# Three products on constant tables ahead of TensorE's wait for the second up matrix of every expert

## The reference

```
def expert_block(args):
    xb, e = args
    hb = jax.nn.silu(xb @ w1[e]) * (xb @ w3[e])
    return hb @ w2[e]
```

## Time and profile before

| | before |
| --- | --- |
| median of three runs | 1366.91 us |
| the profiled execution, its own time | 1372.07 us |
| its span, first to last instruction | 1370.3 us |
| mean granted TensorE clock | 0.956 |
| TensorE busy | 1131.5 us, 83% |
| DMA queue of SyncE | 458.01 MB, 81.6% of 16 engines' span |
| matrix products with up matrices (line 884) | 154.2 + 126.8 us in the two largest groups |

### The profile page before, as it was taken

The page is one execution under the profiler, slowest core; times in us unless marked ns, Lnnn a source line. Parts: engine busy times, 40 slices in busy tenths (PEclk is TensorE's granted clock), DMA queues, the critical chain, the costliest instruction groups (busy, mean ns, idle before and its releaser), DMA issues.

```text
span 1370.3 us, 34053 instructions
## 1 busy us (share of the span) xinstructions
PE 1131.5 (83%) x14903; PEld 712.7 (52%) x14903; DVE 402.2 (29%) x1111; ACT 231.4 (17%) x616; POOL 12.8 (1%) x28
## 2 busy tenths in 40 slices
PE   8999789867767778869999999988987677677794
PEld 4444355544444445548887557445554444454552
DVE  1254522211111111134468735043221111111123
ACT  0133211100000001123533114111110000001011
POOL 0000000000000000020000000000000000000000
PEclk9999999999999999979999999999999999999997
DMA  9924599999999999993335324589999999999995
GB/s 355 377 105 173 233 394 427 427 426 426 426 427 425 428 427 424 424 399 112 118 122 169 106 79 150 226 353 389 423 429 427 424 428 427 424 428 426 425 424 239
DMA packets 63150, 461.36 MB, mean 337 GB/s; under 512 B 3824, under 2 KB 4000, under 8 KB 30320
## 3 DMA queue, kind: packets, MB, share of 16 engines
q1 hardware_dynamic: 62256, 458.01, 81.6%
q0 software_dynamic: 832, 2.46, 0.5%
HBM read 459.41 MB, written 1.05 MB: 336 GB/s over the span
## 4 chain that ended last, share of the span: by engine, by line
PE 47%; DMA 42%; DVE 5%; SPq 2%; ACT 2%; issue 1%; DVEq 0%
DMA ring<-in_moe_w 27%; DMA arena<-in_moe_w 14%; PE bank L884 8%; PE bank L988 8%; PE bank L714 5%; PE bank L1197 4%; PE bank L1063 4%; PE bank L842 3%; PE bank L898 3%; SPq L494 2%; PE bank L865 2%; PE bank L765 2%; ACT arena L1227 1%; PE bank L1153 1%; PE bank L847 1%
## 5 line engine op out<-in xcount | busy, mean ns | idle before, releaser
L884 PE MATMUL bank<-ring,arena 128*32 128x128 f32 x4544 | 154.2, 289 | 104.3 <-DMA ring<-in_moe_w 87.4
L884 PEld LDWEIGHTS bank<-ring,arena 128*32 128x32 f32 x4544 | 135.2, 114 | 120.9 <-DMA ring<-in_moe_w 88.8
L884 PE MATMUL bank<-arena 128*32 128x128 f32 x3520 | 126.8, 302 | 75.4 <-DMA arena<-in_moe_w 67.0
L884 PEld LDWEIGHTS bank<-arena 128*32 128x32 f32 x3520 | 111.0, 118 | 87.4 <-DMA arena<-in_moe_w 60.2
L1227 ACT ACTIVATE arena<-bank 128x256 f32<-128x256 f32 (+4 forms) x179 | 75.6, 424 | 354.3 <-PE bank L855 137.3
L842 PE MATMUL bank<-x,pick 128*32 128x256 f32 x1024 | 130.0, 637 | 0.7 <-DVEq L1689 0.7
L1744 DVE SCALAR_TENSOR_TENSOR gated<-gated,bank 128x128 f32<-128x128 f32 x64 | 18.4, 288 | 379.1 <-ACT gated L1309 379.1
L988 PE MATMUL bank<-xy,ring 128*128 128x256 f32 x512 | 115.7, 384 | 0.0
L988 PEld LDWEIGHTS bank<-xy,ring 128*128 128x128 f32 x512 | 96.9, 192 | 14.6 <-issue 1.6
L898 PE MATMUL bank<-ring,hT 128*32 128x256 f32 x1632 | 98.8, 382 | 0.4 <-ACT hT L1227 0.4
L1309 ACT ACTIVATE gated<-bank 128x128 f32<-128x128 f32 x64 | 17.8, 278 | 441.5 <-PE bank L884 441.5
(11 more groups left out here) (244 smaller groups left out, 956.9 us busy)
## 6 DMA issues: line engine op xcount, KB each, us to landing
ring<-in_moe_w SPq DMA_DIRECT2D x122, 2048.0 KB, 40.5
arena<-in_moe_w SPq DMA_DIRECT2D x66, 2048.0 KB, 40.0
ring<-in_gdn_w_in SPq DMA_DIRECT2D x12, 2048.0 KB, 9.6
ring<-in_ab_w_in SPq DMA_DIRECT2D x5, 2048.0 KB, 21.0
ring<-in_gdn_w_out SPq DMA_DIRECT2D x4, 2048.0 KB, 8.8
held<-in_moe_w SPq DMA_DIRECT2D x2, 2048.0 KB, 19.4
ring<-in_ab_w_out SPq DMA_DIRECT2D x2, 2048.0 KB, 23.8
xy<-in_moe_w SPq DMA_DIRECT2D x2, 2048.0 KB, 14.3
```

Source lines behind the costliest of these rows:

```text
L884: last = mm(psum[5][h * CAP:(h + 1) * CAP, m * FH:(m + 1) * FH], xeT[:, j], slot_tile(slots[m])[:, j, h // 2 * SEQ + h % 2:(h // 2 + 1) * ...
```

## The change

Ahead of the wait for the second up matrix, TensorE gets three products of the identity with the first 384 columns of the constant table, written into bank 6, where nobody reads them. They wait for nothing and signal nothing.

```diff
@@ -668,6 +668,11 @@
             def gdn_ready(u):
                 pe.wait_ge(slot_full[slot_gdn(u)], 16 * GDN_FILL[u])
 
+            def fill_wait(bank, count):
+
+                for _ in range(count):
+                    mm(bank[:, 0:3 * P], ident, const[:, 0:3 * P], start=True, stop=True)
+
             def transpose_x(n, t):
 
                 if n == 0:
@@ -878,6 +883,8 @@
                         pe.wait_ge(s.gpt, n + (2 + s.g))
 
                         for m in range(2):
+                            if m == 1:
+                                fill_wait(psum[6], 3)
                             pe.wait_ge(*filled[m])
                             for j in range(DJ):
                                 for h in range(TILES):
```

## The result

The changed kernel takes 1373.62 us (median of 20 runs, 1369.69 to 1377.86), the kernel before, timed beside it, 1369.38 us (20 runs, 1363.69 to 1372.72). The ratio is 1.0034, 95% interval [1.0023, 1.0045]: slower by a third of a per cent, 4.2 us between the medians and some 4.7 us by the ratio. I had forecast no change, +0.6 us, with 1371.5 as the upper end. The kernel before is itself 2.5 us slower over 20 runs than over the three of the forecast, so the 2.1 us by which the range was missed need not come from the change; the ratio does.

The account below looks back on a forecast made before the run. Transfers were taken to set the end of both expert stages, with TensorE bounding the rest. Middle 0, openings 0.3, closings 0 and 0.3 made +0.6 us on the 1366.91 us median: 1367.5 us, range 1364.0 to 1371.5.

Parts of the forecast that it names:

- What one fill costs: Three 384-column products ahead of the second up product's wait: 1.94 us at full clock, 3.87 us at half.
- The closing turns: Turns 27 to 31: 0 us in layer 0 (0 to +2.0), +0.3 us in layer 1 (-0.8 to +1.6).
- the rival: Behind turn 27 TensorE, not the transfers, sets each layer's end: +5.6 us, 1372.5 us; chance 0.10.
- The opening turns: Later second and third loads behind turn 0: 0 us in layer 0, 0.3 in layer 1, bounds 0 and 1 each.
- the margin was 0.45 us: End of layer 0: time to spare before the last down product would no longer wait for its matrix, 0.45 us.
- The 2.4 us code stall: A TensorE stall for code as in turn 29 of layer 1, which might come in the last turns: 2.4 us.
- my 2.5 us between issue and full flow: Layer 0's start: delay from a load's issue to full transfer, 2.5 us; by it both later loads just make it.
- The clock: Second up products stay at 2.4 GHz, 2.05 us each, worth nothing mid-layer; rival that it pays: 5.0 us faster, chance 0.04.
- the 1.4 us that I had counted in turn 26 of layer 1: Its second product at full clock, 2.05 instead of 3.49 us, would let turn 27 start 1.4 us sooner.
- The middle: Mid-layer turns: the fill fits in the 2.74 us wait, leaving 0.8 us, and costs nothing as DMA sets the pace.
- The longer loop: Added instructions still stay on the core; rival that code is fetched anew: +4 us, 1371 us, chance 0.02.
- The range: Whole kernel: 1364.0 to 1371.5 us, with about 2 in 10 outside; the terms' bounds add to -0.8 and +5.6 us.

Follow-up runs that it names:

- the two changed kernels: The kernel with three products in every turn, run twice against the kernel before: ratios 1.0034 and 1.0036.
- the second trace of the changed kernel: Trace of the repeat of the kernel with three products in every turn, unaltered; ratio 1.0036 to the kernel before.

## Why the prediction was wrong, point by point

**What one fill costs** is the term that failed, and it turned no change into a loss. I took three products in the middle of a turn for three of a long row of equal ones, 1.94 us. They cost 2.24: the second up product starts 4.12 us behind the first instead of 1.87 (541.65 to 545.77). The 0.3 us on top come once per fill, whatever its length (0.96 us for one product, 4.2 for six). The first product of the fill starts 1.98 us behind the up product, and the next up product 2.13 us behind the fill. There TensorE turns from 32-column tiles to the full array and back, and I take that for the cause; it is not shown, as no run had a fill of 32-column tiles. My price came from equal products back to back, and I had given the term no range.

**The closing turns** were the right place with the right mechanism, and the rival named it: chance 0.10. From turn 27 to the last down product my working gives 4 x 12.27 + 5.84 + 1.7 = 56.6 us; measured 58.07, 58.09, 58.06 and 58.07 us in four stages of the two changed kernels. The 1.5 us between are five times 0.3. It is not the transfers that set the later end: the last down matrix of a stage lands 421.7 and 421.2 us behind its start, where before it was 421.1 and 421.2. With 56.6 the stages would have ended within 0.7 us of the landing of the last matrix, with 58.07 they end 1 to 2 us behind it. Worked out from these traces, with 56.6 layer 1 would have ended as before (365.01 + 56.6 = 421.6) and layer 0 0.8 us later (365.41 + 56.6 = 422.0 against 421.24): of the 3.7 us, 2.9 are this term's and 0.8 the opening turns'. In layer 0 the margin was 0.45 us, less than the error of the sum. The 2.4 us code stall, by which the rival came to its price, did not come: all closing turns are 12.55 us. That its +5.6 us lies near the measured 4.7 is luck.

**The opening turns** were sized about right, not exactly: 0 to 1 us a layer forecast, 0 to 1.3 measured, in the first trace in layer 0, to which I had given 0. The reasoning failed, too. The second and third load were issued 6.2 and 11.8 us into the stage, inside the limits of 7.2 and 12.1 us that follow from my 2.5 us between issue and full flow, and up to 1.3 us were lost all the same.

**The clock**: the second products did come at full speed, and the granted clock from 300 to 400 us rose from 0.95 to 0.98, in part because TensorE waits for no matrix there before 380.70 us. But the falls that are left, 7 in the two expert stages where there were 22, begin in the first up product (the second trace of the changed kernel has 7, too), and the last of them took back 0.8 of the 1.4 us that I had counted in turn 26 of layer 1. That a higher clock in the middle is no gain in time was right. "TensorE: Matmul & The Clock Gate" of the Trainium skill, section "HAM oscillation — how this bites in real kernels", says that a wait for DMA in every tile lets the array fall back to the slow clock, and that the remedy is a loop in which it stays at the fast one. This case's traces agree as to the clock (22 falls became 7) and not as to the time, since DMA sets the pace there: 426 GB/s in both.

**The middle** cost nothing, as said: the first up products from 395.55 to 454.50 us, which wait for their matrices, start 14.7 us apart on average, four steps of 14.65 to 14.87. In layer 0 TensorE first waits again at 380.70 us, in turn 16, where before it did in turn 8.

**The longer loop** stays on the core: between 215 and 530 us all packets are data, as the earlier trace rows.

**The range** missed by 2.1 us. The same kernel's median moved up by 2.5 us from three runs to twenty, and I had allowed for such scatter only downwards. (The lower end, by its own terms, is 1367.5 - 0.8 - 2.5 = 1364.2, not 1364.0.) Against the kernel timed beside it the change, 4.2 to 4.7 us, lies inside my bounds of -0.8 to +5.6 us; what failed is the term behind the +0.6.

## What to carry to other kernels

Filler ahead of a wait is free only in turns that have the wait. Where the loads of the first turns, or of one in the middle, are in place beforehand, a stretch of turns runs at the compute engine's pace, and each filler there stands on the path: add them up from the last turn that waits to the end, with a price for each interruption beside that of its products, and compare with the time of the last landing. If the margin is less than the sum's uncertainty, size the filler down: one or two products lost nothing here, and one was even a quarter of a per cent faster, for a reason that stays open.

## What the runs showed of the hardware

A few full-array products between products of 32-column tiles cost 0.3 us beyond their own time (0.645 us each), once per interruption, for one to six products alike. Work ahead of one of two waits left 7 of 22 falls of the granted clock, and these came at the other wait: in two traces of the changed kernel products of 2.6 to 3.6 us appeared behind its 1.9 to 2.0 us of idle time, where the kernel before had none of them. And identical instructions differ by up to 5 us outside the expert stages, with the granted clock from 794 to 806 us at 0.72 in one trace and 1.00 in another, while the stages bound by DMA repeat to 0.5 us. With such a kernel, lengths of stages from two or three traces show a change of 1 to 2 us that a dozen timed runs, with intervals of 0.15% to either side, can't tell from none.
